# Next block's input rows: loaded in column quarters, scaled and turned on the vector engine instead of scaled by ScalarE and turned by TensorE

## The reference, cut to what matters

```
h    = x * rsqrt(mean(x*x) + 1e-6) * pre_g          # per token
proj = h @ w_in                                     # 1024 x 3360, four groups of columns
A: short gated convolution   B: RWKV-7 time mixing   C: latent attention, causal   D: attention on 256 memory tokens
mixed = concat(A,B,C,D outputs, each times silu(its gate))
x = x + rms_norm(mixed @ w_out) * post_g
```

## Time and profile before

| what | value |
|---|---|
| median of 3 runs | 3565.73 us (3564.42 to 3566.42) |
| the profiled execution | 3564.9 us, its span 3563.1 us |
| PE busy | 3445.3 us, 97% |
| DVE busy | 1923.1 us, 54% |
| ACT busy | 1338.2 us, 38% |
| POOL busy | 242.9 us, 7% |
| granted TensorE clock | 0.994 of full speed, mean |

### The profile page before, as it was taken

How to read it: one execution, slowest core, us unless ns; L and a number is a source line. 1 busy time by engine, 2 the same in 40 slices (tenths; PEclk the granted TensorE clock), 3 DMA queues, 4 the chain that set the end, 5 groups by cost and what they waited for, 6 DMA issues and landing times.

```text
span 3563.1 us, 80754 instructions
## 1 busy us (share of the span) xinstructions
PE 3445.3 (97%) x33272; PEld 2619.7 (74%) x33272; DVE 1923.1 (54%) x4974; ACT 1338.2 (38%) x3669; POOL 242.9 (7%) x340
## 2 busy tenths in 40 slices
PE   7999999999999999999999999999999999999998
PEld 5768686877868778686567786868777687776864
DVE  3646465555646546465346465656546464463653
ACT  2333334243343433524423333342433435335343
POOL 3200000000000000000041000000000000000000
PEclk9999999999999999999999999999999999999999
DMA  6654353525435153252355534435163351632511
GB/s 205 208 176 157 140 188 117 187 85 186 136 112 203 51 203 124 102 180 68 114 183 191 189 133 172 156 124 196 58 228 118 115 179 48 237 104 90 191 55 67
DMA packets 268960, 514.56 MB, mean 144 GB/s; under 512 B 28965, under 2 KB 199923, under 8 KB 256051
## 3 DMA queue, kind: packets, MB, share of 16 engines
q1 hardware_dynamic: 247059, 463.72, 38.0%
q0 software_dynamic: 11648, 41.95, 3.3%
q10 hardware_dynamic: 9888, 3.74, 0.4%
HBM read 472.89 MB, written 47.49 MB: 146 GB/s over the span
## 4 chain that ended last, share of the span: by engine, by line
PE 81%; DVE 7%; ACT 6%; issue 3%; DVEq 2%; ACTq 1%; SPq 0%; DMA 0%; POOL 0%; POOLq 0%
PE bank L799 74%; PE bank L803 7%; DVEq L1535 2%; ACT hT L2336 1%; ACT Q L2512 1%; ACTq L2488 1%; ACT L2489 1%; ACT PT L2628 0%; ACT qr L2511 0%; ACT Sm L2585 0%; DVE mix L1595 0%; DVE T L1677 0%; DVE T L1679 0%; DVE pr L1675 0%; DVE mix L1747 0%
## 5 line engine op out<-in xcount | busy, mean ns | idle before, releaser
L799 PE MATMUL bank<-hT,win 128*128 128x256 f32 (+3 forms) x6384 | 1191.8, 340 | 4.6 <-ACT hT L2336 4.5
L799 PEld LDWEIGHTS bank<-hT,win 128*128 128x128 f32 (+1 forms) x6384 | 955.2, 187 | 145.3 <-issue 37.6
L799 PE MATMUL bank<-wout,win 128*128 128x128 f32 x3136 | 379.9, 276 | 0.0
L799 PEld LDWEIGHTS bank<-wout,win 128*128 128x128 f32 x3136 | 364.7, 192 | 1.0
L799 PE MATMUL bank<-kv,Q 96*128 96x512 f32 (+3 forms) x640 | 276.5, 530 | 0.2
L1885 DVE TENSOR_REDUCE ml<-bank 128x1 f32<-128x512 f32 (+3 forms) x320 | 195.5, 611 | 143.5 <-PE bank L799 133.0
L803 PEld LDWEIGHTS bank<-cst,Sm 128*128 128x128 f32 x1344 | 157.6, 140 | 145.0 <-issue 69.2
L803 PE MATMUL bank<-cst,Sm 128*128 128x128 f32 x1344 | 210.6, 278 | 24.8 <-ACT Sm L2585 17.9
L799 PE MATMUL bank<-wout,mix 128*128 128x512 f32 x480 | 220.7, 607 | 10.9 <-ACT hT L2336 8.8
L2585 ACT ACTIVATE Sm<-bank,ml 128x512 f32<-128x512 f32 (+3 forms) x320 | 199.6, 624 | 74.5 <-DVE ml L1890 68.6
L799 PEld LDWEIGHTS bank<-wout,mix 128*128 128x128 f32 x480 | 89.5, 193 | 121.5 <-issue 115.4
(11 more groups left out here) (519 smaller groups left out, 5919.8 us busy)
## 6 DMA issues: line engine op xcount, KB each, us to landing
win<-wfast SPq DMA_DIRECT2D x98, 1024.0 KB, 6.4
win<-in_w_in SPq DMA_DIRECT2D x78, 1024.0 KB, 5.2
win<-wfast SPq DMA_DIRECT2D x98, 768.0 KB, 4.5
wout<-in_w_out SPq DMA_DIRECT2D x60, 512.0 KB, 7.3
out_xres<-xin SPq DMA_DIRECT2D x16, 1024.0 KB
xin<-in_x_prompt SPq DMA_DIRECT2D x15, 1024.0 KB
xin<-out_xres SPq DMA_DIRECT2D x15, 1024.0 KB
win<-in_w_in SPq DMA_DIRECT2D x16, 896.0 KB, 4.8
```

The costliest lines, as they stand in the source:

```text
L799: return pe.matmul(out, lhsT, rhs, start=start, stop=stop, skip_group_check=True)
```

## The change

x of the next block is loaded by four DMAs, one for each quarter of 256 columns, to 32 partitions each: partition 32g + j holds, for t = 0..7, the columns 256g to 256g+255 of token 32t + j. ACT takes the squares in eight pieces (sum_quarters); one matmul with a repeated identity adds the four quarters and spreads the sum (in attention, ahead of tile 24); ACT copies it out (take_sums), POOL makes the roots (row_roots, after the first three gathers). DVE multiplies by root and pre_g (scale_rows, eight pieces, each after the masked maximum of a chunk from number 6 on; what is left over comes after gate(B, 2)). Then, between gate(B, 2) and memory_out, turn_rows writes hT with eight transposes in blocks of 32x32. So partition p of hT now holds the features 8p to 8p+7, and w_in's rows are grouped in the same way. PE's turn_x is left for the first rows of a layer alone. project_out waits for s_mix only ahead of its fifth step (k == 6); in the last block it still does at the head. The bonus moves between take_pair 5 and take_pair 6. The scratch of POOL's DMAs is halved.

The diff, without most of its context:

```diff
...
-VECS = [("pre", 8), ("conv", 6), ("mu", 7), ("w0", 2), ("a0", 2), ("kk", 2), ("ka", 2), ("rk", 2),
+VECS = [("conv", 6), ("mu", 7), ("w0", 2), ("a0", 2), ("kk", 2), ("ka", 2), ("rk", 2),
...
     put("scan", np.broadcast_to((np.arange(T) % C != 0)[None, :] * 1.0, (P, T)))
-    put("rep", (r == q % 32) * 1.0)
+    put("rep", (r % 32 == q % 32) * 1.0)
...
 xin = sb("xin", [P, 2, D])
-st = sb("st", [P, 48])
+st = sb("st", [P, 48]); xsum = sb("xsum", [P, 16])
+gain = sb("gain", [P, 256]); preT = sb("preT", [P, KD])
...
 memT = kv[:, 8192:10240].rearrange("p (k n) -> p k n", k=KD)
+xq = xin[:, :, :].rearrange("p j d -> p (j d)").rearrange("p (t c) -> p t c", c=256)
...
 s_const = sig("const_loaded", 0)
-s_lvl = sig("layer_vectors_loaded", 16 * len(VECS))
+s_lvl = sig("layer_vectors_loaded", 16 * (len(VECS) + 5))
...
 s_fpr = sig("prompt_states_read", 1)
-s_x = sig("x_loaded", 16)
+s_x = sig("x_loaded", 64)
...
         sp.wait_ge(s_vr.h, s_vr.at(l, 0))
-        rows("pre", a["pre_norm_g"][sl, :])
+        sp.dma_start(preT[:, :], a["pre_norm_g"][sl, :].rearrange("a (p k) -> p (a k)", k=KD)).then_inc(s_lvl.h, 16)
+        for g in range(4):
+            sp.dma_start(gain[32 * g:32 * g + 32, :], a["pre_norm_g"][sl, 256 * g:256 * g + 256].broadcast_to([32, 256])).then_inc(s_lvl.h, 16)
...
             if px == l * IT + 2:
-                sp.sem_inc(s_x.h, 16)
-            sp.dma_start(xin[:, :, :], prompt_rows(l, tok)).then_inc(s_x.h, 16)
+                sp.sem_inc(s_x.h, 64)
+            rows = xres[l, tok:tok + T, :] if l else a["x_prompt"][0, tok:tok + T, :]
+            for g in range(4):
+                sp.dma_start(xq[32 * g:32 * g + 32, :, :], rows[:, 256 * g:256 * g + 256].rearrange("(t j) c -> j t c", j=32)).then_inc(s_x.h, 16)
...
             sp.dma_start(xin[0:NS, 0, :], sample_rows(l)).then_inc(s_x.h, 16)
+            sp.sem_inc(s_x.h, 48)
...
         else:
-            sp.sem_inc(s_x.h, 16)
+            sp.sem_inc(s_x.h, 64)
...
             c = GROUPS[TILES[PAIRS[i]][0]][1]
-            rows = a["w_in"][l, :, c:c + P].rearrange("(k p) n -> p k n", p=P)
+            rows = a["w_in"][l, :, c:c + P].rearrange("(p k) n -> p k n", k=KD)
...
             sp.dma_start(wfast[l, i, :, 0:2 * 512].rearrange("p (k n) -> p k n", n=P), rows).then_inc(s_wst[0].h, 16)
-            rows = a["w_in"][l, D // 2:D, c + P:c + 2 * P].rearrange("(k p) n -> p k n", p=P)
+            rows = a["w_in"][l, :, c + P:c + 2 * P].rearrange("(p k) n -> p k n", k=KD)[:, KD // 2:KD, :]
...
             w = 160 if GROUPS[g][0] == "ckv" else w
-            src = a["w_in"][sl, :, c0:c0 + w].rearrange("a (k p) n -> p (a k) n", p=P)
+            src = a["w_in"][sl, :, c0:c0 + w].rearrange("a (p k) n -> p (a k) n", k=KD)
...
         for dt in range(KD):
-            last = tr(PP[bank + dt // 4][:, (dt % 4) * P:(dt % 4 + 1) * P], xn[:, dt * P:(dt + 1) * P], P)
+            last = tr(PP[bank + dt // 4][:, (dt % 4) * P:(dt % 4 + 1) * P], xn.rearrange("p (c k) -> p k c", k=KD)[:, dt, :], P)
...
             scores(c)
+        if B.turns:
+            pe.wait_ge(s_ss.h, s_ss.at(B.px + 1, 1))
+            mm(PP[4][:, 0:8], K("rep"), xsum[:, 0:8]).then_inc(s_xt.h, 2)
...
         w = min(B.n, P)
-        if B.turns:
-            turn_x(B.px + 1, 0, bank=0)
...
             prompt_states(B.l)
-        pe.wait_ge(s_mix.h, s_mix.at(B.ot, 1))
-        if B.prompt:
-            pe.wait_ge(s_uvr.h, s_uvr.at(B.ip, 1))
+            pe.wait_ge(s_mix.h, s_mix.at(B.ot, 1))
+        pe.wait_ge(s_uvr.h, s_uvr.at(B.ip, 1))
...
         for i0, k in enumerate(OUT_ORDER):
-            if B.turns and i0 == 3:
-                turn_x(B.px + 1, 1, bank=2)
+            if k == 6:
+                pe.wait_ge(s_mix.h, s_mix.at(B.ot, 1))
...
         l = B.l
-        if i0 == 1 and B.turns:
-            pe.wait_ge(s_hT.h, s_hT.at(B.px + 1, 1))
...
                 pe.wait_ge(s_sdv.h, s_sdv.at(l, SDV["variance"]))
-                pe.wait_ge(s_hT.h, s_hT.at(B.px + 1, 2))
...
         v.wait_ge(s_pa.h, s_pa.at(B.ip, k))
+    def scale_rows(B, k):
+        if k == 0:
+            v.wait_ge(s_xr.h, s_xr.at(B.px + 1, 2))
+        v.scalar_tensor_tensor(xq[:, k, :], xq[:, k, :], xsum[:, 8 + k:9 + k], gain[:, :], MULT, MULT)
+    def turn_rows(B):
+        v.wait_ge(s_pj.h, s_pj.at(B.ip, NTILES))
+        for k in range(8):
+            last = v.transpose(hT[:, :, 32 * k:32 * k + 32], xq[:, k, :].rearrange("p (i k) -> p k i", k=KD))
+        last.then_inc(s_hT.h, 2)
+        drain()
+        v.tensor_copy(st[:, 47:48], st[:, 46:47]).then_inc(s_xn.h, 2)
...
         h = [[hT[:, a * 4:(a + 1) * 4, j * P:(j + 1) * P] for j in range(2)] for a in range(2)]
-        v.wait_ge(s_hT.h, s_hT.at(B.px + 1, 2))
...
         drain()
+    def bonus(B):
+        n = B.n
+        v.wait_ge(s_sqd.h, s_sqd.at(B.it, 3))
+        v.tensor_tensor(bon[:, :, 0:n], halves(3, n), pr[:, 4:6, 1:1 + n], MULT).then_inc(s_bor.h, 1)
...
             take_pair(B, 5, cxs)
+        bonus(B)
+        if B.fast:
...
         drain()
-    def bonus(B):
-        n = B.n
-        v.wait_ge(s_sqd.h, s_sqd.at(B.it, 3))
-        v.tensor_tensor(bon[:, :, 0:n], halves(3, n), pr[:, 4:6, 1:1 + n], MULT).then_inc(s_bor.h, 1)
...
             v.tensor_tensor(Om[j], An[j], mlev[:, lev + 1:lev + 2, :].broadcast_to([P, NH, 64]), MULT).then_inc(s_om.h, 1)
-        bonus(B)
...
             masked_max(c)
+        scaled = 0
...
             masked_max(c)
+            if B.turns and c > 5 and scaled < 8:
+                scale_rows(B, scaled)
+                scaled += 1
...
         v.tensor_copy(inv64, scalars(rinv, 64)).then_inc(s_on.h, 1)
+        return scaled
...
             rwkv_chunks(B)
-            attention(B, l, m, e)
+            scaled = attention(B, l, m, e)
...
             gate(B, 2, Bp)
+            if B.turns:
+                for k in range(scaled, 8):
+                    scale_rows(B, k)
...
             drain()
+            if B.turns:
+                turn_rows(B)
...
             else:
-                act.wait_ge(s_x.h, s_x.at(px, 16))
+                act.wait_ge(s_x.h, s_x.at(px, 64))
...
             act.drain()
+        def sum_quarters(px):
+            act.wait_ge(s_x.h, s_x.at(px, 64))
+            for t in range(8):
+                if t == 4:
+                    act.drain()
+                last = act.activation(flat3(OO)[:, (t % 4) * 256:(t % 4 + 1) * 256], xq[:, t, :], ACT.Square, accum_out=xsum[:, t:t + 1])
+            last.then_inc(s_ss.h, 1)
+        def take_sums(px):
+            act.wait_ge(s_xt.h, s_xt.at(px, 2))
+            act.activation(xsum[:, 8:16], PP[4][:, 0:8], ACT.Copy).then_inc(s_ss.h, 1)
...
             for dt in range(KD):
-                last = act.mul(hT[:, dt, cols], PP[bank + dt // 4][:, (dt % 4) * P:(dt % 4) * P + w], V("pre", dt))
+                last = act.mul(hT[:, dt, cols], PP[bank + dt // 4][:, (dt % 4) * P:(dt % 4) * P + w], preT[:, dt:dt + 1])
...
             if B.turns:
-                sum_squares(B.px + 1)
+                sum_quarters(B.px + 1)
...
             rwkv_out(2)
-            if B.turns:
-                act.wait_ge(s_sur.h, s_sur.at(ip, 2))
-                normalise(B.px + 1, 0)
...
                     take_tile(B, 24, mix[:, 5, :])
+                    if B.turns:
+                        take_sums(B.px + 1)
...
             variance_root(B)
-            if B.turns:
-                take_h(B.px + 1, 0, tile_cols(0), bank=0)
-                normalise(B.px + 1, 1)
-                take_h(B.px + 1, 1, tile_cols(1), bank=2)
...
             pool.tensor_tensor(st[:, 4 + j:5 + j], st[:, 4 + j:5 + j], mhalf[:, :], POW).then_inc(s_xr.h, k)
+    def row_roots(px):
+        pool.wait_ge(s_ss.h, s_ss.at(px, 2))
+        pool.tensor_scalar(xsum[:, 8:16], xsum[:, 8:16], 1.0 / D, EPS, MULT, ADD)
+        pool.drain()
+        pool.tensor_tensor(xsum[:, 8:16], xsum[:, 8:16], mhalf[:, :].broadcast_to([P, 8]), POW).then_inc(s_xr.h, 2)
...
                     weight_sums(B, i)
-            if B.turns:
-                x_roots(B.px + 1)
...
                 gather(B.block, q)
+            if B.turns:
+                row_roots(B.px + 1)
...
     from concourse.bass_utils import run_bass_kernel_spmd
-    nc = bacc.Bacc("TRN2", target_bir_lowering=False, num_devices=1, dynamic_dma_scratch_size=4096)
+    nc = bacc.Bacc("TRN2", target_bir_lowering=False, num_devices=1, dynamic_dma_scratch_size=2048)
...
```

## The result

The changed kernel takes 3574.58 us (median of 9 runs, 3572.05 to 3580.93), the one before, beside it, 3564.34 (9 runs, 3560.49 to 3568.89). The ratio is 1.0031, interval 1.0021 to 1.0042: 0.31% slower, about 10 us. The profiled execution took 3576.5 us, its span 3574.7. The forecast was 3549, with a range of 3537 to 3571.

The account below looks back on a forecast made before the run. PE, busy 97% of the span, was taken as the bound. Block-end and bonus gains of 19.9 us, less 1.6 start, 1.0 first rows and 1.4 scalings, gave 15.9: from 3564.9 to 3549 us, range 3537 to 3571.

Parts of the forecast that it names:

- Bonus, 7.3 us: Bonus product ahead of the last take_pair: PE's waits for bon in 14 fast blocks go, gain 7.3 us.
- Blocks 4 to 6, 17.1: Ends of blocks 4 to 6, six cases: DVE has cover, PE gains 2.85 us each, together 17.1.
- Transposes at 0.40 each: Eight DVE transposes at a block's end, 0.40 us each (ends 0.30 and 0.76), the strided read taken as free.
- The idle clock: PE's waits at the ends of blocks: the prediction counted their length and had no term for the clock.
- Scalings between maxima, 1.4: DVE's row scalings between score maxima in the attention: 0.1 us a block lost, 1.4 us in all.
- Loads, priced at nothing: Regrouped w_in rows, x loads in pieces, and the fifth projection step's weights: no cost charged.
- Start 1.6: Layer 0's start: four more vector-load issues at 0.40 us delay PE's first instruction, 1.6 us lost.
- First rows 1.0: First rows still turned on PE: 48 transposes whose weights are read every eighth element, 1 us lost.
- the late root: Rival, attention: POOL's power takes 2.94 us, DVE stands 1.3 us at the first scaling; 3566 us; chance 0.12.
- slow transposes: Rival, block ends: DVE transposes take 0.76 us each, blocks 0 to 3 pay 23 us; 3572 us; chance 0.17.

Follow-up runs that it names:

- the filled run: Changed kernel with 8, 6 and 3 unused matmuls in front of PE's hand-over waits in blocks 0, 1 and 2 to 3: 3563.7 us, 0.9997 against before.

## Why the prediction was wrong

What each edit does was named rightly. The sign was lost in one size, and in an effect that the sum does not have, PE's clock after a wait. By its steps:

- **Bonus, 7.3 us: right.** 9 measured, interval 6 to 13.
- **Blocks 4 to 6, 17.1: right.** 16.7.
- **Transposes at 0.40 each: wrong, 0.54 apart.** This is the first step that failed, a term of the sum that was mis-sized: 1.1 us more in eight hand-overs, 9 us. I reasoned from the reduce in PSUM that a strided read is free. It is not, from SBUF: 0.60 us against 0.41 at a stride of 32 bytes. The rule of the Trainium skill that I set against the change ("SBUF — State Buffer", "Door 1: The DMA port swizzle", 16-byte lines) pointed the right way, and this trace agrees with it in sign; the page gives no price.
- **The idle clock: absent.** This is the second step that failed, a term put at nothing. I priced a wait of PE at its length. A wait of 5.4 us or more was forecast for block 0 and 4.6 for block 1, and the earlier trace rows stood in front of a stretch at half clock that I did not look at. Filling the waits gave 12 us back. The Trainium skill has this in "TensorE: Matmul & The Clock Gate", section "HAM oscillation — how this bites in real kernels": after a wait for data the clock is low, and half of the throttled time is lost. This trace agrees: PE was busy at the lower level for 24 us more than before, half of that is 12, and the filled run gave 12 back.
- **Scalings between maxima, 1.4: right but for block 0.** POOL's power was forecast at 1.7 us and took 1.68. But between it and the operation before it POOL stood still, which the sum left out: for 1.54 and 1.11 us in block 0 of the two layers, for 0.56 in the other twelve blocks. The root was late in block 0 alone, at 188.0 in layer 0. Why POOL stood longer there is open. 6 us with the clock, where I had 0.1 a block.
- **Loads, priced at nothing: wrong by up to 5.7 us.** Waits of PE for w_in's loads (3.4 us) and for wout (2.3) are new. The regrouping is not the cause; what is stays open.
- **Start 1.6: right** (1.3). **First rows 1.0** can't be told apart in the traces.

The forecast missed the span by 11.6 + 15.9 = 27.5 us, and the transposes, the idle clock and the late root come to 9 + 12 + 6 = 27. That they meet so closely is partly luck. Each was measured in another kernel and is good to about 5 us; the stretch at half clock in block 0's attention of layer 0, part of the 6, is gone in the filled run too, so it is counted twice; and the 5.7 us of new waits for loads are in none of them. What the runs do show is that the transposes' price and the clock behind the waits are the two large terms.

The rival "slow transposes" named the mechanism and the right blocks, but put its break-even at 0.65 us each; that its time, 3572, came close is luck, since it took 0.76 each and no clock. The runs put the break-even near 0.40, on a straight line between two of them: at 0.34 apart the kernel is 5 us faster than before, at 0.54 it is 11 slower. That is the price I had taken; at it the change as ordered gains nothing, because the clock and the late root had been left out.

## What to carry to other kernels

Before work is moved to an engine with idle time, look for what stands behind the new place in that engine's queue and who waits for it: here the same work was 10 us slower than before in one order and 44 faster in another, of which 28 came only with it. A wait of the matmul engine costs its length, and it can cost half-speed matmuls behind it as well, as eight of the ten waits for kv of 2 to 7.5 us at the ends of blocks 0 to 3 did here, before and after; read the granted clock around such waits in the kernel before. A stall that goes shows the next one in the same queue, so go on until the window shows the engine busy throughout.

## What the runs showed of the hardware

- A DVE transpose in 32x32 blocks of 128x256 fp32 takes 0.41 us from a contiguous source and 0.60 from one read every eighth element, 0.34 and 0.54 apart in a row of eight.
- PE busy with useless matmuls through its waits made the kernel 12 us faster than PE idle. Of four waits of 2.9 us at one place in the code, two were followed by matmuls at half clock and two were not.
- A power on POOL of 8 columns took 1.68 us, and 0.56 us passed between the operation before it and its start in twelve blocks, 1.11 and 1.54 in the two others.
